# Inversion of two token tiles in a gated DeltaNet layer: the tiles shifted by half a level, one stretch of four dense matmuls a level

## What is computed

```python
A = jnp.where(strict, bc[..., :, None] * kk * dmat, 0.0) + jnp.eye(C, dtype=kk.dtype)
u = lax.linalg.triangular_solve(A, bc[..., None] * vc, left_side=True, lower=True, unit_diagonal=True)
w = lax.linalg.triangular_solve(A, bc[..., None] * kc * jnp.exp(G)[..., None],
                                left_side=True, lower=True, unit_diagonal=True)
```

## Time and profile before

| | us |
|---|---|
| median of 3 executions | 1829.7 (1828.36 to 1830.35) |
| profiled execution | 1829.64 |
| its span | 1827.8 |
| TensorE matmuls busy | 1772.2, 97% of the span |
| VectorE busy | 967.5, 53% |
| ScalarE busy | 521.4, 29% |

### The profile page before, as it was taken

The page is one execution under the profiler, slowest core; times in us unless marked ns, Lnnn a source line. Parts: engine busy times, 40 slices in busy tenths (PEclk is TensorE's granted clock), DMA queues, the critical chain, the costliest instruction groups (busy, mean ns, idle before and its releaser), DMA issues.

```text
span 1827.8 us, 28684 instructions
## 1 busy us (share of the span) xinstructions
PE 1772.2 (97%) x10974; PEld 1262.9 (69%) x10974; DVE 967.5 (53%) x2308; ACT 521.4 (29%) x1167; POOL 90.8 (5%) x133
## 2 busy tenths in 40 slices
PE   7999999999999999999999999999999999999999
PEld 5777788775655577776467777888756555776763
DVE  2749665545765556433137596555457654545421
ACT  3142413014366522100112424020144664211000
POOL 0000201001200000000000002010111000000000
PEclk9999999999999999999999999999999999999999
DMA  6312312124531146544042233020255211554421
GB/s 204 115 46 70 98 48 41 30 64 125 150 86 35 36 117 189 157 159 145 0 165 70 69 70 98 25 47 25 64 147 149 64 35 52 164 169 116 159 75 40
DMA packets 196526, 170.01 MB, mean 93 GB/s; under 512 B 49249, under 2 KB 186899, under 8 KB 195943
## 3 DMA queue, kind: packets, MB, share of 16 engines
q1 hardware_dynamic: 192164, 150.11, 28.5%
q0 software_dynamic: 4064, 18.03, 3.0%
q10 hardware_dynamic: 162, 0.05, 0.0%
HBM read 153.66 MB, written 21.71 MB: 96 GB/s over the span
## 4 chain that ended last, share of the span: by engine, by line
PE 79%; DVE 12%; issue 3%; ACT 3%; SPq 2%; DMA 1%; ACTq 0%; POOL 0%; DVEq 0%
PE PS L947 52%; PE PS L876 6%; DVE arena L1898 3%; PE PS L1327 2%; PE PS L1340 2%; DVE arena L1823 2%; PE PS L1396 1%; PE PS L1167 1%; PE PS L1149 1%; PE PS L1169 1%; DVE ws L1829 1%; PE PS L1053 1%; SPq L664 1%; PE PS L1181 1%; DVE arena L1902 1%
## 5 line engine op out<-in xcount | busy, mean ns | idle before, releaser
L947 PE MATMUL PS<-hT,ring 128*128 128x288 f32 x2384 | 629.9, 409 | 6.2 <-ACT sg L1580 3.2
L947 PEld LDWEIGHTS PS<-hT,ring 128*128 128x128 f32 x2384 | 440.2, 190 | 134.0 <-issue 11.0
L947 PE MATMUL PS<-tt,ws 128*128 128x288 f32 x736 | 205.6, 412 | 8.8 <-DVE sg L1956 4.4
L947 PE MATMUL PS<-zs,owr 128*128 128x288 f32 x768 | 209.1, 413 | 2.5 <-DVE sg L1829 1.5
L947 PEld LDWEIGHTS PS<-zs,owr 128*128 128x128 f32 x768 | 137.9, 190 | 48.7 <-issue 12.4
L947 PEld LDWEIGHTS PS<-tt,ws 128*128 128x128 f32 x736 | 133.0, 190 | 51.8 <-DVE sg L1956 8.0
L876 PE MATMUL PS<-con,arena 128*128 128x128 f32 (+5 forms) x950 | 145.7, 279 | 13.5 <-DMA arena<-in_nsa_k_norm 10.9
L876 PEld LDWEIGHTS PS<-con,arena 128*128 128x128 f32 (+5 forms) x950 | 109.3, 140 | 70.9 <-issue 42.4
L1826 DVE TENSOR_TENSOR sg<-PS,sg 128x288 f32<-128x288 f32 x140 | 63.9, 457 | 131.1 <-PE PS L947 125.3
L947 PE MATMUL PS<-arena 128*128 128x512 f32 (+1 forms) x320 | 124.8, 593 | 2.1 <-DVE sg L1956 2.1
L1577 ACT ACTIVATE sg<-PS 128x288 f32<-128x288 f32 x46 | 18.7, 407 | 316.2 <-PE PS L947 316.2
(11 more groups left out here) (316 smaller groups left out, 2096.4 us busy)
## 6 DMA issues: line engine op xcount, KB each, us to landing
ring<-in_w_in SPq DMA_DIRECT2D x54, 1024.0 KB, 5.4
arena<-in_cache_nsa_kv SPq DMA_DIRECT2D x128, 192.0 KB, 2.7
ring<-in_w_in SPq DMA_DIRECT2D x32, 256.0 KB, 4.6
arena<-in_state_nsa_win SPq DMA_DIRECT2D x32, 256.0 KB, 3.4
arena<-in_cache_nsa_kv SPq DMA_DIRECT2D x128, 64.0 KB, 1.8
arena<-in_w_out SPq DMA_DIRECT2D x4, 2048.0 KB, 8.3
out_win_sample<-in_state_nsa_win POOLq DMA_DIRECT2D x2, 4032.0 KB, 23.0
arena<-in_x_prompt SPq DMA_DIRECT2D x8, 512.0 KB, 5.3
```

The source lines that it names most:

```text
L947: ins = mm(to, w, x, start=start, stop=stop, skip_group_check=True)
```

## The change

The two tiles of a group go half a level apart. A level on TensorE is now: lower product of tile 0, side products of tile 1 of the level before, side products of tile 0, lower product of tile 1, then one `fill(4)`. Level 1 keeps a `fill(2)` in place of the missing piece, and behind level 6 stand the last side products of tile 1 and a `fill(2)`: a group takes 6 + 5 x 4 + 2 = 28 dense matmuls where it took 24. VectorE goes in the same order: mask 0, subtraction 1 of the level before, subtraction 0, mask 1. The single sample tile keeps its order, and no arithmetic changes. On line numbers of the changed kernel, 1149 is 1150, 1145 is 1146, 1163 is 1166, 1167 and 1169 are 1170 and 1172, and 1823, 1826 and 1829 are 1839, 1842 and 1845.

```diff
+                    def below(lev, li):
...
+                        pe.wait_ge(s["i_xm"], past["i_xm"] + n_ix + (lev - 2) * len(group) + li + 1)
...
+                    def beside(lev, li):
...
+                        pe.wait_ge(s["i_wm"], past["i_wm"] + n_iw + (lev - 1) * len(group) + li + 1)
...
                     for lev in range(1, levels):
-                        sz = 1 << lev
-                        for li, k in enumerate(group):
...
-                            pe.wait_ge(s["i_xm"], past["i_xm"] + n_ix - len(group) + li + 1)
...
-                        fill(2, u0 + U_MG0)
-                        for li, k in enumerate(group):
...
-                            pe.wait_ge(s["i_wm"], past["i_wm"] + n_iw + li + 1)
...
-                        fill(2, u0 + U_MG0)
+                        below(lev, 0)
+                        if len(group) == 2 and lev > 1:
+                            beside(lev - 1, 1)
+                        else:
+                            fill(2, u0 + U_MG0)
+                        beside(lev, 0)
+                        if len(group) == 2:
+                            below(lev, 1)
+                        fill(2 * len(group), u0 + U_MG0)
+                    if len(group) == 2:
+                        beside(levels - 1, 1)
                         fill(2, u0 + U_MG0)
...
                     for lev in range(1, levels):
-                        sz = 1 << lev
-                        for li, k in enumerate(group):
...
+                        masked(lev, 0)
+                        if len(group) == 2 and lev > 1:
+                            less(lev - 1, 1)
+                        less(lev, 0)
+                        if len(group) == 2:
+                            masked(lev, 1)
+                    if len(group) == 2:
+                        less(levels - 1, 1)
```

More of the change, by code:

```diff
@@ new lines, in beside @@
+                    def beside(lev, li):
+                        n = TILES[group[li]][1]
+                        Y, half = xy(li, n, 1), n // 2
+                        sz = 1 << lev
+                        pe.wait_ge(s["i_wm"], past["i_wm"] + n_iw + (lev - 1) * len(group) + li + 1)
+                        for h in range(DN_H):
+                            w = tmp["W"][0:n, li, h, 0:n]
+                            new = [PS[0:n, 4 + li, (x * DN_H + h) * half:(x * DN_H + h + 1) * half]
+                                   .rearrange("p (a c) -> p a c", c=sz) for x in range(2)]
+                            if sz == n // 2:
+                                ins = mm(new[1], w, blocks(Y[:, h], sz, 1), start=True, stop=True)
+                                continue
+                            if lev < levels - 1:
+                                for m in diagonal(n):
+                                    mm(new[0][m], Y[m, h, m], blocks(w[m], sz, 0), start=True, stop=True)
+                            for m in diagonal(n):
+                                ins = mm(new[1][m], w[m, m], blocks(Y[m, h], sz, 1), start=True, stop=True)
+                        step("i_x")
+                        ins.then_inc(s["i_x"], 1)
@@ L1176, in _ @@
+                    n_iw += (levels - 1) * len(group)
+                    n_ix += (levels - 1) * len(group)
                     if TILES[group[0]][0] < SEQ:
@@ new lines, in masked, with less @@
+                    def masked(lev, li):
+                        n = TILES[group[li]][1]
+                        count = n_iw + (lev - 1) * len(group) + li + 1
+                        take_before("i_w", count)
+                        dve.wait_ge(s["i_w"], past["i_w"] + count)
+                        mul(tmp["W"][0:n, li, :, 0:n], bank4(2 + li, n, n), rep(C("lev", P, k=lev)[0:n, 0:n], DN_H))\
+                            .then_inc(s["i_wm"], 1)
+                    def less(lev, li):
+                        n, sz = TILES[group[li]][1], 1 << lev
+                        count = n_ix + (lev - 1) * len(group) + li + 1
+                        new = xy_new(li, n, sz)
+                        prod = PS[0:n, 4 + li, 0:DN_H * n].rearrange("p (x a c) -> p x a c", x=2, c=sz)
+                        if lev == levels - 1:
+                            new, prod = new[:, 1], prod[:, 1]
+                        take_before("i_x", count)
+                        dve.wait_ge(s["i_x"], past["i_x"] + count)
+                        sub(new, new, prod).then_inc(s["i_xm"], 1)
@@ new lines, in _ @@
+                    for lev in range(1, levels):
+                        masked(lev, 0)
[6 more added lines that the diff above has]
+                        less(levels - 1, 1)
+                    n_iw += (levels - 1) * len(group)
+                    n_ix += (levels - 1) * len(group)
```

59 lines of the change are left out of this document (13 added, 46 removed).

## The result

| | before | changed |
|---|---|---|
| median, us | 1830.29 (5 runs, 1828.36 to 1831.48) | 1838.33 (5 runs, 1836.75 to 1839.34) |
| profiled execution, us | 1829.64 | 1838.33 |
| its span, us | 1827.8 | 1836.3 |
| TensorE busy, us | 1772.2 | 1773.7 |
| VectorE busy, us | 967.5 | 976.3 |

The ratio is 1.0044, 95% interval 1.0032 to 1.0057. The forecast was 1824.8 with a range to 1832.0, so the time lies outside and on the other side. Two numbers in the table are a lead. VectorE does the same operations and is busy 8.8 us longer.

The account below looks back on a forecast made before the run. TensorE's instruction stream (busy 97%) and its waits for other engines were taken as the bound. The terms summed to -2.5 us a layer, -4.9 in two layers from 1829.64: 1824.8 us, range 1819.0 to 1832.0.

Parts of the forecast that it names:

- Fewer switches: Inversion: seven tiled stretches for ten a group, three pairs of switches less at 0.32 or 0.33 each; -2.0 us a layer.
- Ordinary waits: Ordinary inversion levels: TensorE waits 0.06 to 0.1 for tile 0's mask, three to four levels a group; +0.5 us a layer.
- The rival in which every eviction delays tile 0's mask: Inversion: mask 0 starts 0.5 later at six levels a layer, +6 in all, 1830.8 us; chance 0.08.
- Heavy level: One inversion level a group: mask 0 behind unit "5"'s eviction and three sums, wait 1.7 to 1.75 twice; +3.4 a layer.
- Waits that go: Inversion and building: level 1 -0.55, level 4 of second group -0.9, second group's building -0.35, before sample tile -0.8.
- fourth group: Before the sample tile's first lower product: the 0.76 wait behind VectorE goes as the sums move away; -0.8 us a layer.
- State steps and norms: After the inversions: idle times of 0.23, 0.38 and 1.58 all go, ScalarE's roots not late; -2.5 us a layer.
- the time that the prediction worked out with a drain: Norms: about 1.38 us extra per ScalarE table switch would use up the roots' 2.6 to spare; sum 1827.6 us.
- Rotary products: Four stalls on VectorE evictions, 2.5 us a layer together, partly go; -0.6 a layer, bounds -1.5 and +0.5.
- Attention: Middle of the attention: the same stalls for the softmax remain; 0 us a layer, bounds -1.5 and +1.5.
- Tail: Attention's last slots: matmuls taken early are missing as cover, 1.3 of 1.94 returns as wait; +1.3, bounds 0 and 1.9.
- The rival "slower": Mask queued behind the sums decides while vanished stalls may reappear at the next unit; 1834 us, chance 0.16.

Follow-up runs that it names:

- after_again: The changed kernel run once more, unaltered, on the same chip as the kernel before: 1837.76 us, ratio 1.0034 to the kernel before.
- a_sums_behind: Changed kernel with the weight sums of the inversion's levels held until tile 1's mask is done: 1834.03 us against 1831.22 before, ratio 1.002.
- a_pool_late: Changed kernel with GpSimd's four state multiplies started only after VectorE's two state-step subtractions: 1827.71 us against 1831.22 before, ratio 0.9988.

## Why the prediction was wrong

*Fewer switches, -2.0 a layer*: right. 2.14 for eight dense loads, and 0.35 a level between the ordinary levels of before and after. The shift by itself, waits included, gave 1.7 a layer.

*Ordinary waits, +0.5*: 0.08 in the level looked at, as forecast. The rival in which every eviction delays tile 0's mask did not come about: in that level the eviction is done before the mask starts, at the 0.73 that the prediction gave. *Heavy level, +3.4*: 1.75 as worked out in the first group, but 0.78 in the second, where I had used the first group's phase of the stream; +2.5. *Waits that go*: building -0.48 for -0.35, fourth group -0.80 for -0.8. Up to the sample tile the sum was -1.92, counted from the first level, where I had -0.7: the best-known part of it was too pessimistic by 1.2, of which 0.9 is the heavy level of the second group.

*State steps and norms, -2.5*: **the step that failed.** The waits that I listed did go (-2.30 from the state update to the sums of squares). But I wrote "the stream is two units further on here" and asked only which of TensorE's waits that takes away, and that "nothing is late next" with ScalarE's roots in mind. I did not move VectorE's own jobs along: unit "5" brings 1.9 us of sums, and by two units they come into GpSimd's 7.5 us of multiplies and ahead of the two subtractions that TensorE needs. That costs 6.02 in the first layer and 6.94 in the second: 4.65 of standstill, and the matmuls at half clock. In the first layer 4.65, the transposes' 0.46 (1.06 for 0.60) and the dense matmuls' 1.09 (3.20 for 2.11), less the 0.23 of idle time that goes, make 5.97. The place was to be seen in the trace of before, in the POOL row that I hadn't read, 0.04 us ahead of the first sum. Its price was not: the weight sums that run beside GpSimd in that trace take 0.68 to 0.74, so its rows would have said that such an overlap costs next to nothing.

The roots were not late, and the table loads took 1.28 with their users right behind (445.79 and 447.08, 449.59 and 450.89), so the time that the prediction worked out with a drain did not come; by its own terms it is about 1827.8 and not 1827.6. The forecast's own sum, twice -2.5, gives 1824.6 before rounding. Neither changes an argument.

*Rotary products, -0.6*: -1.0 where the clock does not fall, +0.68 where it does. The prediction put the stalls there at 2.5; TensorE's rows in the trace of before have 0.72, 0.73 and 0.59, 2.0 in all. *Attention, 0 with bounds of 1.5*: +2.11 and +0.53 (`after_again`), in both +2.0 for the sums ahead of a softmax step in the first slots and -1.5 behind them; the difference is the fall of the clock. *Tail, +1.3*: +1.16.

The rival "slower" gave 1834 and was nearer than the forecast, but by a wrong cause. Its mechanism, the mask behind the sums, cost 5 us in all, which the rest of the inversion pays for, and `a_sums_behind` shows that without it the kernel is still slower. Its other half, that a stall of VectorE's queue reappears at the next unit, was the right thought without a place: it should have been asked at each step that VectorE does for TensorE, with a list of the sums' new neighbours. Forecast and rivals alike left TensorE's clock alone, and each of the standstills of 4.65 and 5.25 here brought a fall of it.

## What to carry to other kernels

Moving filler work moves everything that hangs on it, on every engine. For each long job that rides along, list what it will stand ahead of and what runs beside it, GpSimd included; an idle engine's row is quickly read. Four dense matmuls fewer at one place, weight sums made a little later and one semaphore wait on GpSimd turned +0.4% into -0.8%, with the same arithmetic.

## What the hardware showed that I had not expected

A VectorE `tensor_tensor` on 128x512 with both inputs in SBUF took 1.97 to 2.40 us beside GpSimd's 128x1024 multiplies in place of 0.69 (one of the six in the rows above took 1.00), while each of those went from 1.88 (7.52 for four) to 2.1 (8.42): the one engine pays about threefold, the other 12%. Evictions from PSUM are not touched (0.46 beside the multiplies and elsewhere). Beside GpSimd's 128x128 `tensor_scalar` the same sums took 0.68 to 0.74.

In a standstill of TensorE of 4.65 us the granted clock fell to its lower level, 1.2 GHz, in both layers of both profiles of the changed kernel, and so it did in one of 5.25; behind waits of 0.7 to 2 us it fell in some executions and not in others, which is likely why the runs of one kernel spread by up to 11 us here (`a_pool_late`, 1823.9 to 1835.3). The mean granted clock of the fastest of those runs is 1.000 and of the slowest 0.995. That last was not tried by itself.
